# adaLN groups 3 to 5 as running sums on VectorE, with one short TensorE sum per group

## What is computed

```python
silu_c = jax.nn.silu(c)
silu_cc = jax.nn.silu(c_ctx)
for l in range(DEPTH):
    mod = (silu_c @ w_ada[l] + b_ada[l])[:, None, :]      # 1024 -> 6144
    sh1, sc1, gt1, sh2, sc2, gt2 = jnp.split(mod, 6, axis=-1)
    mod_c = silu_cc @ w_ada[l] + b_ada[l]
    h = modulate(rmsnorm(x, g_mix[l]), sh1, sc1)
    ...  # attention and convolution groups, one output projection
    x = x + gt1 * merge_groups(a_out, cv_out, g_attn_out[l], g_conv_out[l], w_out[l])
    h2 = modulate(rmsnorm(x, g_ffn[l]), sh2, sc2)
    x = x + gt2 * swiglu(h2, w_gate_up[l], w_down[l])
    ...  # the context stream likewise, in layer 0 only
```

## Time and profile before

| what | value |
|---|---|
| median of 3 runs | 1657.31 us (1656.78 to 1658.14) |
| the profiled execution's own time | 1658.43 us |
| its span, first to last instruction | 1656.1 us |
| PE busy | 1570.3 us, 95% of the span |
| DVE busy | 837.1 us, 51% |
| ACT busy | 570.1 us, 34% |
| chain that ended last: PE's share | 84%, of which line 465 71% and line 412 2% |
| mean granted TensorE clock | 0.981 |
| DMA | 161.19 MB, mean 97 GB/s |

### The profile page before, as it was taken

One profiled execution on the slowest core, in us unless ns is written; L12 is line 12 of the kernel. 1 busy time (PEld: TensorE's weight loads), 2 busy tenths in 40 slices (PEclk: granted clock), 3 DMA queues, 4 the chain that ended last, 5 costly groups with the idle time before them and its releaser, 6 DMA issues.

```text
span 1656.1 us, 25043 instructions
## 1 busy us (share of the span) xinstructions
PE 1570.3 (95%) x9804; PEld 1278.1 (77%) x9804; DVE 837.1 (51%) x1527; ACT 570.1 (34%) x882; POOL 126.3 (8%) x162
## 2 busy tenths in 40 slices
PE   3899987999999999999999999988999999999997
PEld 0675654578888878888788878765578998998995
DVE  1484566867433322433233455767776443443445
ACT  2411258734443111221122233136845541321222
POOL 0032012021000000000000000521120000000000
PEclk9999988999999999999999999998999999999998
DMA  8474420002112442124412353511012223323222
GB/s 325 178 219 107 177 91 1 1 26 65 56 59 63 165 153 64 63 63 139 171 60 63 104 199 104 144 52 39 1 39 90 89 90 100 89 89 100 91 76 88
DMA packets 39865, 161.19 MB, mean 97 GB/s; under 512 B 5616, under 2 KB 6000, under 8 KB 33648
## 3 DMA queue, kind: packets, MB, share of 16 engines
q1 hardware_dynamic: 35856, 148.72, 26.7%
q0 software_dynamic: 3936, 11.45, 2.6%
HBM read 149.76 MB, written 2.10 MB: 92 GB/s over the span
## 4 chain that ended last, share of the span: by engine, by line
PE 84%; DVE 7%; ACT 4%; issue 2%; DMA 2%; SPq 1%; POOL 0%; DVEq 0%; ACTq 0%; POOLq 0%
PE banks L465 71%; PE banks L494 3%; PE banks L572 2%; PE banks L584 2%; PE banks L599 2%; PE banks L412 2%; DMA x<-in_xT 1%; PE banks L452 1%; PE banks L435 1%; DVE w_low L949 1%; ACT prob L765 1%; DVE ssum L956 1%; DMA raw<-in_w_mix 0%; ACT w_high L684 0%; DVE row_max L1048 0%
## 5 line engine op out<-in xcount | busy, mean ns | idle before, releaser
L465 PE MATMUL banks<-h_high,w_high 128*128 128x512 f32 (+1 forms) x1856 | 433.3, 315 | 5.0 <-DVE h_low L978 3.5
L465 PE MATMUL banks<-h_high,w_low 128*128 128x512 f32 (+1 forms) x1856 | 428.8, 313 | 0.0
L465 PE MATMUL banks<-h_low,w_high 128*128 128x512 f32 (+1 forms) x1856 | 428.6, 312 | 0.0
L684 ACT ACTIVATE w_high<-raw 128x1024 fp32r<-128x1024 f32 (+1 forms) x178 | 185.5, 1042 | 672.8 <-PE banks L465 664.5
L949 DVE TENSOR_TENSOR w_low<-raw,w_high 128x1024 fp32r<-128x1024 f32 (+1 forms) x178 | 217.6, 1222 | 238.7 <-ACT w_high L684 236.6
L465 PEld LDWEIGHTS banks<-h_high,w_high 128*128 128x128 f32 x1856 | 289.0, 190 | 40.1 <-issue 18.8
L465 PEld LDWEIGHTS banks<-h_low,w_high 128*128 128x128 f32 x1856 | 288.4, 190 | 21.6
L465 PEld LDWEIGHTS banks<-h_high,w_low 128*128 128x128 f32 x1856 | 287.3, 190 | 21.6
L992 DVE COPY shift_product<-banks 128x2 f32<-128x2 f32 x116 | 18.4, 159 | 354.0 <-PE banks L465 342.2
L465 PE MATMUL banks<-ff_high,w_high 128*128 128x512 f32 (+1 forms) x528 | 162.5, 362 | 0.5 <-DVE ff_low L1287 0.5
L465 PE MATMUL banks<-ff_low,w_high 128*128 128x512 f32 (+1 forms) x528 | 160.0, 357 | 0.0
(11 more groups left out here) (147 smaller groups left out, 1582.9 us busy)
## 6 DMA issues: line engine op xcount, KB each, us to landing
raw<-in_w_gu SPq DMA_DIRECT2D x88, 512.0 KB, 3.5
ada_raw<-in_w_ada SPq DMA_DIRECT2D x21, 1024.0 KB, 5.1
raw<-in_w_dn SPq DMA_DIRECT2D x32, 512.0 KB, 3.6
raw<-in_w_mix SPq DMA_DIRECT2D x28, 512.0 KB, 5.5
ada_in_ff<-in_w_ada SPq DMA_DIRECT2D x12, 1024.0 KB, 5.0
raw<-in_w_out SPq DMA_DIRECT2D x16, 512.0 KB, 3.6
ada_first<-in_w_ada SPq DMA_DIRECT2D x7, 1024.0 KB, 13.5
raw<-in_w_dn SPq DMA_DIRECT2D x16, 384.0 KB, 3.0
```

The costliest lines, as they stand in the source:

```text
L465: last = mm(bank[:, 2 * slot + bk, 0:b - a], weights[w][:, k0_w + k, :], rhs[:, k0_rhs + k, a:b], start=(k == 0 and n == 0), stop=(k == kt ...
L684: f(wH[j][:, 0:k, :], raw[j][:, 0:k, :], ACT.Copy).then_inc(w_high, 1)
```

## The change

Groups 0 to 2 stay as they are. The units of groups 3, 4 and 5 leave PE. They now stand in `gu0`, `gu1` and `dn1` of layer 0 on DVE: for each unit and each of the two condition vectors, one instruction over 128x2048 multiplies the tile by that vector's entry for the partition and adds it to a running sum (for k = 0 only multiplies). The two sums lie in `w_conv` and in `ada_sum_context`, which takes the place of `ssum` and the `sq` tiles, idle there. When a group is complete, PE adds the partitions of both sums by eight matmuls with `pick_stream` standing still (a 128x32 tile with one column of ones), in the second block of `dn0`, `dn1` and `gu2`, and transposes in the same block. Written-out and looped code changes place: PE's `dn0`, `dn1`, `dn2` of layer 0 become loops, DVE's `gu0`, `gu1` and `dn1` of layer 0 are written out, and DVE and ACT take the first pair out of the other FFN loops of both layers. The release of the ada buffers is now counted by `ada_read`.

```diff
+        ada_sums = [ada_in_qkv, ada_sum_ctx[:]]
-        ada_row = act_out[:, 0:AGW // 4]
+        ada_row = [act_out[:, 0:AGW // 4]] * 3 + [scratch[:, 0:AGW // 4]] * 3
+        pick = sb("pick_stream", [P, 2, 32])
-        ADA_IN = {(0, "u"): 1, (0, "qkv"): 2, (0, "dn0"): 3, (0, "dn1"): 4, (0, "dn2"): 5}
-        TURN_IN = {(0, "qkv"): 1, (0, "gu1"): 3, (0, "gu2"): 4, (1, "u"): 5}
+        ADA_IN = {(0, "u"): 1, (0, "qkv"): 2, (0, "gu0"): 3, (0, "gu1"): 4, (0, "dn1"): 5}
+        ON_PE = ("u", "qkv")
+        SUM_IN, TURN_IN = {(0, "dn0"): 3, (0, "dn1"): 4, (0, "gu2"): 5}, {(0, "qkv"): 1}
-            at = (0, 1, 1, 2, 3, 3, 4, 5) if name == "qkv" else [k * (blocks - 1) // (DT - 1) for k in range(DT)]
+            at = (0, 1, 1, 2, 3, 3, 4, 5) if name == "qkv" else [blocks // DT * k for k in range(DT)]
-                last_use[place] = g * DT + k + 1
+                last_use[place] = (ada_mm, g * DT + k + 1) if g < 3 else (ada_read, units_before((g, k)) + 1)
...
+            def ada_sum(g):
+                pe.wait_ge(ada_read, DT * (g - 2))
+                for v in range(2):
+                    for q in range(4):
+                        last = mm(bank[32 * q:32 * q + 32, ADA, :], pick[:, v, :], ada_sums[v][:, 512 * q:512 * q + 512],
+                                  start=(v == 0), stop=(v == 1), tile_position=(0, 32 * q))
+                last.then_inc(ada_mm, 1)
...
+                if (layer, name) in SUM_IN:
+                    g = SUM_IN[layer, name]
+                    after[1].append((1, lambda: ada_sum(g)))
+                    after[1].append((DT - 2, lambda: ada_turn(g)))
...
+            def ada_multiply(unit):
+                g, k = unit
+                tile, landed, count, _ = ADA_PLACES[unit]
+                dve.wait_ge(landed, count)
+                if k == 0:
+                    dve.wait_ge(ada_mm, 3 * DT + g - 3)
+                else:
+                    dve.wait_ge(ada_read, units_before(unit))
+                for v in range(2):
+                    if k == 0:
+                        last = ts(ada_sums[v], tile, cond[:, k, v:v + 1], None, ALU.mult)
+                    else:
+                        last = stt(out=ada_sums[v], in0=tile, scalar=cond[:, k, v:v + 1], in1=ada_sums[v],
+                                   op0=ALU.mult, op1=ALU.add)
+                last.then_inc(ada_read, 1)
...
                         scale_product(0, context)
                         split_low(layer, gu, i, 0)
+                        if isinstance(i, int):
+                            for u in ada_units(layer, gu, 2 * i):
+                                ada_multiply(u)
...
                             update(layer, j, i + USES[layer, dn], 5, t, context)
+                            if isinstance(i, int):
+                                for u in ada_units(layer, dn, 2 * i + j):
+                                    ada_multiply(u)
...
+            nc.gpsimd.memset(pick[:], 0.0).then_inc(consts, 1)
+            pool.wait_ge(consts, 4)
+            for v in range(2):
+                nc.gpsimd.memset(pick[:, v, v:v + 1], 1.0)
```

More of the change, by code:

```diff
@@ L352, in load_ada @@
                 if free:
-                    sp.wait_ge(ada_mm, free)
+                    sp.wait_ge(*free)
                 if unit == (ADA_IN[0, "qkv"], 1):
@@ L419, in ada_turn @@
                 for j in range(4):
-                    last = nc.tensor.transpose(bank[:, SMALL, P * j:P * j + P], ada_row[:, P * j:P * j + P], ident[:])
+                    last = nc.tensor.transpose(bank[:, SMALL, P * j:P * j + P], ada_row[g][:, P * j:P * j + P], ident[:])
                 last.then_inc(ada_tr, 1)
@@ L501, in phase @@
                 pairs = PAIRS_OF[name]
-                with_ada = (layer, name) in ADA_IN
+                with_ada = (layer, name) in ADA_IN and name in ON_PE
                 after = {0: [], 1: []}
+                if (layer, name) in SUM_IN:
+                    g = SUM_IN[layer, name]
+                    after[1].append((1, lambda: ada_sum(g)))
+                    after[1].append((DT - 2, lambda: ada_turn(g)))
                 if key is not None:
@@ L513, in phase @@
                                    after[j] if i == 0 else ())
-                        for u in ada_units(layer, name, 2 * i + j):
-                            ada_unit(u)
+                        if with_ada:
+                            for u in ada_units(layer, name, 2 * i + j):
+                                ada_unit(u)
                         if (name, 2 * i + j) in CONV_AFTER:
@@ L718, in ada_rows @@
             def ada_rows(g):
-                act.wait_ge(ada_mm, DT * (g + 1))
+                act.wait_ge(ada_mm, DT * min(g + 1, 3) + max(g - 2, 0))
                 if g == 1:
                     act.wait_ge(z_ok, CT)
-                f(ada_row, bank[:, ADA, :], ACT.Copy).then_inc(ada_rowed, 1)
+                f(ada_row[g], bank[:, ADA, :], ACT.Copy).then_inc(ada_rowed, 1)
             def ada_after(layer, name):
-                if (layer, name) in ADA_IN:
+                if (layer, name) in ADA_IN and name in ON_PE:
                     ada_rows(ADA_IN[layer, name])
@@ L891, in _, with gu_pair @@
                     ff = layer * FT + sum(CHUNKS[:c])
-                    def gu_pair(i):
+                    def gu_pair(i, first=False):
                         split_high(layer, gu, i, 0)
@@ L898, in gu_pair @@
                         last.then_inc(gate_ok, 1)
+                        if first and (layer, gu) in SUM_IN:
+                            ada_rows(SUM_IN[layer, gu])
                         split_high(layer, gu, i, 1)
@@ L901, in gu_pair, with dn_pair @@
                         f(aH[:, i, 0:width], tmp[1][:, 0:width], ACT.Copy).then_inc(ff_high, 1)
-                    with act.Fori(0, tiles - 1) as i:
+                    gu_pair(0, first=True)
+                    with act.Fori(1, tiles - 1) as i:
                         gu_pair(i)
                     gu_pair(tiles - 1)
-                    def dn_pair(i, more=True):
+                    def dn_pair(i, more=True, first=False):
                         for j in range(2):
@@ L910, in dn_pair @@
                                 split_high(layer, dn, i, j)
+                            if first and j == 0 and (layer, dn) in SUM_IN:
+                                ada_rows(SUM_IN[layer, dn])
                             if c == 2:
@@ L926, in _ @@
                     if c < 2:
-                        with act.Fori(0, PAIRS_OF[dn] - 1) as i:
+                        dn_pair(0, first=True)
+                        with act.Fori(1, PAIRS_OF[dn] - 1) as i:
                             dn_pair(i)
@@ L1189, in _ @@
                         taps(10 * i - 5, 10 * i + (i == 3))
-                    if layer and i == 0:
-                        ada_columns(ADA_IN[0, "dn2"])
                 for i in range(3):
@@ L1288, in gu_pair @@
                         dve.wait_ge(ff_low, i + (ff + 1))
-                    with dve.Fori(0, tiles - 1) as i:
+                    apart = tiles - 1 if (layer, gu) in ADA_IN else 1
+                    for i in range(apart):
                         gu_pair(i)
+                        if i == 0 and (layer, gu) in SUM_IN:
+                            ada_columns(SUM_IN[layer, gu])
+                    if apart < tiles - 1:
+                        with dve.Fori(apart, tiles - 1) as i:
+                            gu_pair(i)
                     gu_pair(tiles - 1)
@@ L1317, in _ @@
                         chain.link(nc.vector.memset(ssum[:, 0:width], 0.0))
-                    with dve.Fori(0, PAIRS_OF[dn] - 1) as i:
+                    apart = PAIRS_OF[dn] - 1 if (layer, dn) in ADA_IN else 1
+                    for i in range(apart):
                         dn_pair(i)
+                        if i == 0 and (layer, dn) in SUM_IN:
+                            ada_columns(SUM_IN[layer, dn])
+                    if apart < PAIRS_OF[dn] - 1:
+                        with dve.Fori(apart, PAIRS_OF[dn] - 1) as i:
+                            dn_pair(i)
                     dn_pair(PAIRS_OF[dn] - 1, more=(layer, c) != (DEPTH - 1, 2))
```

18 lines of the change are left out of this document (10 added, 8 removed).

## The result

The changed kernel takes 1634.92 us (median of 4 runs, 1633.91 to 1635.65) against 1657.72 for the kernel before (4 runs); the ratio is 0.9863, with a 95% interval from 0.9846 to 0.988. That is 22.8 us less; by the interval, 20 to 26. Beside each other in the last group of experiments, the unaltered changed kernel (`e_control`) took 1634.31 and the kernel before 1656.72 us, 22.4 apart. The forecast was 1637.0, with a range of 1633 to 1642.5. The profiled execution spans 1633.5 us, 22.6 less than before. One execution among them all, of `e_small_units`, took 2547.95 us at a mean granted clock of 0.591 and enters no comparison.

A forecast was written before the change was run, and what follows sets the result against it. PE's own instructions were taken to bound the kernel: from the profiled 1658.4 us, 26.9 off for 23 units and 6.5 on for three sums gave 1638.0, or 1637 as the median, 1.1 lower; range 1633 to 1642.5.

The forecast's parts named there:

- PE is the bound, its units come back in full: In `dn0` PE is busy 67.00 of 67.00 us, so PE work taken away comes back in full as time.
- A unit 1.17, a sum 2.17: On PE in layer 0, each of 23 counted units removed saves 1.17 us; each of three sums costs 2.17.
- The last unit is free: Behind the last block of `dn2` the unit is worth nothing; without it PE idles some 2.5 us.
- DVE 4.8 us a unit, hidden in `gu`: In `gu0` and `gu1` a unit takes DVE 4.8 us, with 6.05 us free, so it costs no time.
- SP's queue in `dn1`: Unit loads in `dn1` hold back raw blocks until 8.2 us after a block's end, at a cost of zero.
- rival (a): Low-clock stretch at the layer's end grows, losing 3 to 4 us (1641), or goes away (1634); chance 0.15.
- The range: 1633 to 1642.5, some 0.87; ends also called the terms' bounds: sum 1.17 or 3 us, unit 1.10 to 1.26.
- Rival (b): DVE or SP's queue too slow: DVE paces PE beyond 6.0 us a unit in `dn1`, 9.0 in `gu`; chance 0.04.

The follow-up runs named there:

- e_small_units: Changed kernel with DVE's instructions for k = 1 to 7 cut from 2048 to 128 elements, as plain multiplies; 1635.88 us.
- e_sums_twice: Changed kernel with each of PE's three sums of eight matmuls issued twice in a row; 1640.97 us.
- e_group5_on_pe: Changed kernel with group 5's units back on PE in `dn2` of layer 0 and its transpose in layer 1's `u`; 1639.94 us.
- e_tail_unit: Changed kernel with four more matmuls of a unit's shape, result unused, on PE behind the last block of `dn2`; 1634.99 us.
- e_raw_ahead: Changed kernel with SP's loads of the group-5 units issued one block later, in `dn1` and `gu2` of layer 0; 1636.17 us.
- e_act_loops: Changed kernel with ACT's `gu` and `dn` loops of layer 1 beginning at pair 0 again, as in the kernel before; 1636.22 us.
- e_double_dn: Changed kernel with DVE's wide instructions of every group-5 unit, in `dn1`, issued twice; 1665.88 us.
- e_double_dn_raw_ahead: Changed kernel with DVE's group-5 wide instructions issued twice and SP's loads of the group-5 units one block later; 1655.53 us.

## Why the prediction was right, point by point

**PE is the bound, its units come back in full:** right. The earlier trace rows said it, and the edits of PE's work in these stages came out near their own length (`e_sums_twice` 4.85 us for 5.2 in the chain, `e_group5_on_pe` 4.6 for 5.0).

**A unit 1.17, a sum 2.17:** right as a net. From the end of `dn0`'s first block to that of `dn1`'s, before (560.60 to 773.19) and after (562.06 to 767.53, both ends two feature tiles later), the gain is 7.12 us; 8 x 1.17 - 2.17 = 7.19 was the forecast. The pitches after the change part the two: 9.62 - 8.48 and 7.51 - 6.36 give about 1.15 for a unit, and 8 x 1.14 - 7.12 gives about 2.0 for a sum, of which 1.85 to 1.92 show in the chain. Both prices were a little too high, and the errors all but cancel: 23 x 1.15 - 3 x 2.0 = 20.4.

**The last unit is free:** right, by `e_tail_unit`.

**DVE 4.8 us a unit, hidden in `gu`:** right (4.69), by `e_small_units`; the point at which it would pace PE was put at 9.0 and lies near 9.5 by the estimate above.

**SP's queue in `dn1`, "Zero":** wrong, and the one step that failed. I worked out one load of a unit ahead of a raw block, 14 us behind a block's end. At the end of `dn1` two loads stand there in a row, units 6 and 7, and the second waits for unit 5, a block later. The raw block came 5.7 us after ACT wanted it. I had granted that a late split would still be hidden by PE's block of slack; most was, and 1.30 us remained (`e_raw_ahead`, `e_small_units`). The expected 20.0 us of the stage (20.4 less the transpose that moved in) became 18.46; the 0.2 beyond the stall have no cause on record.

**The clock at the layer's end, rival (a):** the loss did not come. The profiled execution gained some 1.65 us there instead. But the length of the half-clock stretch varied between kernels with the same idle time before it (statistics matmuls of 1.50, 1.50, 2.67 and 2.72 us behind 2.5 us of idle), so no run ties a gain or a loss to the change.

**What the sum had no term for:** 1.12 us in layer 1 from ACT's table loads, shown by `e_act_loops`. I had read the written-out first pairs as a cost at most. With the clock's 1.65 and 0.65 at the start of the program, which is within the scatter there, they cover the stall and bring 22.6 against 20.4. That the time came out 2 us below the forecast and not above it is luck, then: the stall that I had at zero is hidden by gains of which the sum had none.

**The range:** its two ends do not come out of the bounds of the terms as I said. With 23 units and three sums these give 1631.8 (1.26 and 1.17) and 1641.1 (1.10 and 3).

**Rival (b), slower through DVE:** the mechanism is real. At 9.4 us a unit in `dn1` it comes to a loss of 8 x 3.4 = 27. `e_double_dn` lost 31 in the median and 28.4 between `gu0`'s statistics and the end of layer 0. The pace alone was less than I had it, 22.6 (`e_double_dn_raw_ahead` against `e_raw_ahead`, 591.58 and 569.03); the queue's order, which I had left out, made up for it.

## What to carry to other kernels

When PE is busy all the time, moving a matmul of poor use (32 of 128 columns) to an engine with room gives back its pitch, read between repeats of the same block, not its busy time. It holds only while the other engine's work fits into each block: at 9.4 instead of 4.7 us a unit in `dn1` the whole gain was gone. Then check the queues: a load that waits for a new, slower reader also holds every load behind it, most of all where two such loads meet at a phase's edge. Gains of 1 us are to be looked for between events of one stage; in the medians the clock's stretches hide them.

## What the runs showed of the hardware that was not expected

The place of a loop's first pass decides where activation-table loads stand: 28 loads of 1.28 us on the FFN's lines before, 2 after the first pair was written out, with the same functions in the same order on ACT, and 15 on lines 707 and 920 when layer 1's loops were put back (`e_act_loops`).

Half clock after a gap: idle times of 1.39 and 2.57 us were both followed by a stretch at half clock, of different length from kernel to kernel, and filling the gap removed it. The same program, the kernel before, took between 1651.4 us at a mean granted clock of 0.985 and 1658.7 at 0.981; what sets when the stretches fall stays open.

The Trainium skill ("VectorE: DVE Perf Modes", "The perf-mode tier table") has float32 `tensor_scalar` in SBUF at twice the rate of `tensor_tensor`; the trace agrees for this form with two tensors and a scalar, 1.28 against 2.35 us at 2048 elements, a factor of 1.83.
